# A decoder layer on one core: the parameters' transfer moved from SyncE's queue to ScalarE's

## The reference, cut to what matters

```python
mod = jax.nn.silu(c) @ w_ada + b_ada                 # c: one row of 1024
shift, scale, gate = jnp.split(mod, 3, axis=-1)
h = rmsnorm(x, g_norm) * (1.0 + scale[:, None, :]) + shift[:, None, :]
proj = h @ w_in                                      # 1024 -> 4096 columns
q, k, v, z_attn, b_g, c_g, h_c, z_conv = jnp.split(proj, splits, axis=-1)
q, k = rope(q, positions), rope(k, positions)
y_attn = rmsnorm(moba_attention(q, k, v), g_attn_out) * jax.nn.silu(z_attn)
y_conv = rmsnorm(short_gated_conv(b_g, c_g, h_c, w_conv), g_conv_out) * jax.nn.silu(z_conv)
y = jnp.concatenate([y_attn, y_conv], axis=-1) @ w_out
out = rmsnorm(x + gate[:, None, :] * y, g_final)
```

## Time and profile before

| what | value |
|---|---|
| median of three runs | 262.08 us |
| the profiled execution's own time | 261.85 us |
| its span, first to last instruction | 259.5 us |
| time around the span | 2.35 us |
| granted TensorE clock over the span | 0.995 |
| TensorE busy | 248.9 us, 96% |
| first head matmul starts | 14.45 us |

### The profile page before, as it was taken

The page is one execution under the profiler, slowest core; times in us unless marked ns, Lnnn a source line. Parts: engine busy times, 40 slices in busy tenths (PEclk is TensorE's granted clock), DMA queues, the critical chain, the costliest instruction groups (busy, mean ns, idle before and its releaser), DMA issues.

```text
span 259.5 us, 3580 instructions
## 1 busy us (share of the span) xinstructions
PE 248.9 (96%) x1188; PEld 203.4 (78%) x1188; DVE 215.1 (83%) x345; ACT 139.1 (54%) x230; POOL 133.6 (51%) x104
## 2 busy tenths in 40 slices
PE   4999999999999999999999999999999999999991
PEld 1478887888888888888888788888888887888880
DVE  5799999799499975997999699963799789996454
ACT  6765665656378460594554575178683561212343
POOL 2520000396716564536199585918479297781240
PEclk9999999999999999999999999999999999999997
DMA  6999996499614785095954438484236992000124
GB/s 241 383 405 423 419 423 262 182 347 290 221 61 131 233 243 163 4 357 164 286 159 141 150 92 248 115 252 144 86 83 157 349 405 100 0 3 0 49 114 162
DMA packets 17827, 52.19 MB, mean 201 GB/s; under 512 B 2577, under 2 KB 7313, under 8 KB 16530
## 3 DMA queue, kind: packets, MB, share of 16 engines
q1 hardware_dynamic: 17520, 51.71, 58.6%
q10 hardware_dynamic: 290, 0.27, 0.3%
HBM read 40.43 MB, written 2.10 MB: 164 GB/s over the span
## 4 chain that ended last, share of the span: by engine, by line
PE 88%; DVE 3%; DMA 2%; ACT 2%; POOL 1%; issue 1%; SPq 0%; POOLq 0%; DVEq 0%
PE ps L1156 22%; PE ps L1158 22%; PE ps L1157 22%; PE ps L1241 5%; PE ps L1306 3%; PE ps L1264 2%; PE ps L1256 2%; DMA xt<-in_x 2%; DVE ya_lo L1082 2%; PE ps L1322 2%; PE ps L1254 2%; PE ps L1262 2%; PE ps L1315 2%; ACT x_junk L382 1%; POOL w_hi L683 1%
## 5 line engine op out<-in xcount | busy, mean ns | idle before, releaser
L690 POOL TENSOR_TENSOR w_lo<-raw,w_hi 128x512 fp32r<-128x512 f32 x58 | 89.7, 1573 | 85.9 <-ACT w_hi L404 50.4
L1156 PE MATMUL ps<-h_lo,w_hi 128*128 128x512 f32 x200 | 78.4, 392 | 0.0
L1158 PE MATMUL ps<-h_hi,w_hi 128*128 128x512 f32 x200 | 78.0, 390 | 0.0
L1157 PE MATMUL ps<-h_hi,w_lo 128*128 128x512 f32 x200 | 77.9, 389 | 0.0
L1156 PEld LDWEIGHTS ps<-h_lo,w_hi 128*128 128x128 f32 x200 | 37.5, 188 | 8.0
L1158 PEld LDWEIGHTS ps<-h_hi,w_hi 128*128 128x128 f32 x200 | 37.5, 188 | 8.0
L1157 PEld LDWEIGHTS ps<-h_hi,w_lo 128*128 128x128 f32 x200 | 37.6, 188 | 7.5
L404 ACT ACTIVATE w_hi<-raw 128x1024 fp32r<-128x1024 f32 x29 | 30.3, 1050 | 7.1 <-DMA raw<-in_wslots 7.1
L494 ACT ACTIVATE probs<-probs,rmin 128x384 f32<-128x384 f32 (+3 forms) x32 | 17.5, 550 | 13.9 <-DVE rmin L944 13.9
L944 DVE CUSTOM_DVE_ANT_0 probs<-mask,ps 128x384 f32<-128x384 f32 (+3 forms) x32 | 13.4, 482 | 7.0 <-PE ps L1306 7.0
L500 ACT ACTIVATE pt_hi<-pt_raw 128x1280 fp32r<-128x1280 f32 x8 | 10.2, 1275 | 11.0 <-DMA pt_raw<-probs 11.0
(11 more groups left out here) (157 smaller groups left out, 486.4 us busy)
## 6 DMA issues: line engine op xcount, KB each, us to landing
raw<-in_wslots SPq DMA_DIRECT2D x33, 512.0 KB, 4.6
ada<-in_ada SPq DMA_DIRECT2D x10, 1024.0 KB, 12.5
pt_raw<-probs SPq DMA_DIRECT2D x32, 160.0 KB, 3.0
raw<-in_whead SPq DMA_DIRECT2D x7, 448.0 KB, 10.8
xt<-in_x SPq DMA_DIRECT2D x4, 512.0 KB, 5.3
ada<-in_ada SPq DMA_DIRECT2D x4, 512.0 KB, 9.3
qd<-qt SPq DMA_DIRECT2D x16, 128.0 KB, 4.0
kd<-kt SPq DMA_DIRECT2D x16, 128.0 KB, 3.1
```

The source lines that it names most:

```text
L690: ins = nc.gpsimd.tensor_tensor(lo[:, half], src[:, half], hi[:, half].bitcast(F32), ALU.subtract)
L1156: nc.tensor.matmul(o, a_hi, b_lo, start=start, stop=False)
L1157: nc.tensor.matmul(o, a_lo, b_hi, start=False, stop=False)
L1158: return nc.tensor.matmul(o, a_hi, b_hi, start=False, stop=stop)
```

## The change

One line leaves the sync block and appears in the scalar block, behind the transfer of c and ahead of the wait for it. All else is the same; who waits for `prm_in` and for `c_in` is unchanged.

```diff
@@ block.sync
-            sp.dma_start(prm[:, :], prm_d).then_inc(prm_in, 16)
             for m in range(TT):
                 sp.dma_start(xt[:, m, :], x[m * P:(m + 1) * P, :]).then_inc(x_in[m], 16)
@@ block.scalar
             nc.scalar.dma_start(crow[0:1, :], c).then_inc(c_in, 16)
+            nc.scalar.dma_start(prm[:, :], prm_d).then_inc(prm_in, 16)
             act.wait_ge(c_in, 16)
             nc.scalar.activation(crow[0:1, :], crow[0:1, :], ACT.Silu).then_inc(c_silu, 1)
```

## The result

| kernel | median of 20 runs | ratio to before, 95% interval | profiled span | first head matmul |
|---|---|---|---|---|
| before | 261.78 us | | 259.5 us | 14.45 us |
| changed | 263.50 us | 1.0056 (1.0042 to 1.0070) | 260.9 us | 16.30 us |

What follows compares the result with a forecast made beforehand. Bound: waits from x's tile 2 through ScalarE and GpSimd to TensorE's first head matmul. Branches x -0.25, TensorE -0.05 to -0.25, VectorE -0.05; the latest, -0.05, takes 261.85 to 261.8, stated as median 262.0 us, range 261.2 to 263.0.

Steps and rivals of the forecast that it cites:

- What bounds the kernel, and that the end follows the head start: TensorE is busy from 14.45 us on, so the end moves only as much as the first head matmul.
- x and SyncE's queue, 0.25 earlier: SyncE's queue: 0.45 us issue slot goes, about 0.2 lost to prm's bytes; x lands 0.25 earlier, bounds 0.15 and 0.45.
- ScalarE, 0.45: ScalarE's second issue before the table load costs 0.45 us, so the silu ends at 4.08 instead of 3.63.
- TensorE's branch, sine transposes at 10.1: TensorE's prologue: broadcast 0.45 us later, sine transposes at 10.1 instead of 10.05; the branch gains 0.05 to 0.25.
- VectorE, prm at 3.8, at most 4.4: VectorE's angle chain: prm lands at 3.8 us, between 3.2 and 4.4; sharing with x adds at most 1.3.
- The trace had no two loaded queues, so it did not decide: DMA queues: the old trace has no stretch with two loaded queues, so it cannot settle prm's landing.
- The break-even at 3.9, by VectorE's own queue: VectorE before `scale_x(2)`: prm landing after 3.9 us costs time against the kernel before, one to one.
- Rival 2: DMA: x's full queue starves prm, landing at 4.4 to 5.2; VectorE decides, +0.5 to +1.3 us; chance 0.12.
- rival 3: TensorE's rate doubles only after the first head chunk begins; TensorE starts 1.2 to 1.6 us later; chance 0.06.
- the landing near 4: DMA queues: by packet round-robin prm's rows go in one turn behind x's share, landing near 4 us, just past break-even.

Runs made afterwards that it cites:

- second issue alone: Kernel before, with ScalarE also issuing a second copy of prm's 50 KB into a spare tile behind c, prm itself unmoved: ratio 0.9999.
- two-unread runs: Changed kernel, and kernel before with angles waiting for x's tile 1, each with added unread TensorE matmuls of 384 and 512 columns: ratios 1.0045 and 1.0085.

## Why the prediction was wrong, step by step

- *What bounds the kernel, and that the end follows the head start.* Right in kind. 1.85 us at the head start became 1.42 at the end; I had said that nothing behind would change.
- *x and SyncE's queue, 0.25 earlier.* Under-sized. Tile 0 landed at 4.0 (4.8 before), tile 2 at 7.75 (8.31 before): 0.56 to 0.7. x's first row moved 0.50 earlier, at 1.73 instead of 2.23, so the whole slot arrived. No branch could use it.
- *ScalarE, 0.45.* Right: 0.37 for the issue, silu at 2.98, broadcast at 4.18 (forecast 4.2). *TensorE's branch, sine transposes at 10.1.* Right where it can be seen, in the kernel with the second issue alone: 10.16, head start 14.39, ratio 0.9999.
- *VectorE, prm at 3.8, at most 4.4.* This step failed. I had two delays, the share of one whole tile and the alternation with x's rows, 1.3 us each, and took them as two descriptions of one wait ("is the same 1.3"). They are one after the other, and prm landed at 5.64. Adding my two terms would have given 3.2 + 1.3 + 1.3 = 5.8, but that is near partly by luck: the wait for the first row measured 1.65, and the alternation 0.72, because the 1.9 that I started from already holds 0.53 for the rows. I also took the middle between them and nothing, on the ground that x had run for only half a microsecond; the spare copy in the kernel before shows 4.4 us to landing although x was issued only 0.13 ahead.
- *The trace had no two loaded queues, so it did not decide.* True, and the right answer was a wide bound. I closed it at 4.4, where the sum of my own two terms was 5.8.
- *The break-even at 3.9, by VectorE's own queue.* The two-unread runs give 4.3, and there the late angles decide through ScalarE's sines and GpSimd, for which I had 4.5. I had called that path covered and looked no further. One to one from 3.9 would give 1.74 us at the head start for a landing at 5.64, close to the 1.85 measured, yet it was made up otherwise: VectorE's first sums were 1.33 later and did not decide.
- *Rivals.* Rival 2 (prm starved) is what happened, past its own end of 5.2, with a part of rival 3 on top: TensorE idled because of VectorE and kept its half rate to about 14.6. I had priced the two as separate cases; the first brings on the second. Rival 3 by itself, priced at 1.2 to 1.6 us, did not show its price in the kernel without the unread matmul, where the rate doubled behind the head start and the time changed by less than 0.7. They had 0.12 and 0.06.

On the Trainium skill (DMA: Bandwidth & Descriptors, Queues, rings and completion order): the round-robin between queues was the warning in the text. By the Trainium skill a DMA engine drains a whole packet, typically 9 to 17 descriptors, from one queue before it switches. The first wait of the changed kernel is of that size: 184 rows and 16 closing packets of x, 12.5 per engine, pass ahead of prm. With x issued 0.13 us ahead or in the same moment only 29 and 32 rows passed, which is less. The one turn for all of prm's rows did not come at all: its 144 packets passed among 136 of the other queue. The measurement decides, and prm landed 1.6 us later than the landing near 4 that I drew from that rule.

## What to carry to other kernels

A small transfer that a long serial chain waits for belongs ahead of the bulk in issue order, across all queues: in this kernel a queue of its own did not let it overtake. Price the wait for its first row and the alternation of its rows with the bulk's as two terms that are added, not as the larger of the two. When an engine's slack is counted, follow every chain that hangs on it: here, with TensorE at its full rate, the sines and GpSimd behind them held the head start, and not VectorE's own queue. And count what its lateness does to the next engine's idle time: a late VectorE here also kept TensorE slow.

## What the runs showed of the hardware

A transfer of one 4 KB row, issued behind 50 KB of small rows on its own queue and 0.44 us behind a 512 KB transfer on another, took 3.44 us. The same 50 KB took 1.8 to 1.9 us ahead of x, 3.0 behind one tile on the same queue, and 3.9 to 4.4 on the second queue, once 6.3; it took 2.8 where x's first rows were of 1 KB. Issued 0.56 us behind x, its first row moved after 184 of x's rows of 4 KB and after 183 of 1 KB; issued 0.13 behind or together with x, after 29 and 32. The granted clock reached 1.00 at 11.04 us in the kernel before, at 12.31 with a second issue alone, at 13.07 with an early unread matmul and at 14.87 without the unread matmul, and the times of the last three did not differ from the first beyond their intervals.
